# Moving two thirds of the mixers' early output product beside the second linear attention

## The chip, the cores and the metric

One core of one Trainium2 chip runs the whole program. The metric is device time in microseconds (us) of one execution; below is better. The engines in play are TensorE (PE, matmuls; PEld are its weight loads), VectorE (DVE), ScalarE (ACT), GpSimd (POOL) and SyncE (SP, which issues the weight loads from HBM).

## What is computed

A block of 512 tokens by 1024 features passes two attention and retention layers, a feed-forward, a layer of token mixers, a second feed-forward and a last norm. The change lies in the mixer layer only. Cut to what matters:

```
p_pool, p_hg, p_rw, p_gla = split(u @ w_in)
y_pool  = multiscale pooling(p_pool)            # 256 columns
y_hgrn  = chunked gated linear attention(p_hg)  # 256 columns, then norm and gate
y_rwkv  = rwkv7_scan(...)                       # 256 columns, then norm, bonus, gate
y_gla   = chunked gated linear attention(p_gla) # 256 columns, then norm and gate
x       = x + concat(y_pool, y_hgrn, y_rwkv, y_gla) @ w_out
```

The last line is a 512 x 1024 by 1024 x 1024 product. It splits over its contraction: each y contributes 256 of the 1024 rows of w_out, and the four contributions may be added to x at different times.

## The kernel before, in words

x is kept feature-major in eight tiles of 128 x 512. Every large product is done in three passes (`three_passes`, L447 to L450): operand and weight are each split in a rounded high part and a low rest, and high by high, low by high and high by low are summed in one PSUM bank of 128 x 512. Weights come in units of 128 x 1024 at most: SP loads one into a ring of four raw buffers, ACT writes its high part, DVE its low part, into rings of three. `use()` on ACT and DVE splits units up to two ahead of the one in use, and a unit's slot comes free when PE has signalled `weights used`.

The eight PSUM banks are handed out by turn in `take` (L417): a product takes the next bank in the turn, and PE waits there until the work named in `freed_by` has emptied it. So a slow reader of one bank stops PE eight takes later, whatever PE would do next.

Each engine has its own instruction stream, which runs in program order. The streams are written side by side with generators: a stage calls `fill(n)` at fixed points, and each engine advances the same generator there.

The mixer layer goes: projections for the pooling and the first attention (`hgrn`); `linear_attention("hgrn", fill_hgrn)`, with the second attention's (`gla`) projections as fillers; `linear_attention("gla", fill_gla)`; `inverse`; `recurrence`. A linear attention has nine levels (`ORDER` = 32, 16, 8, 4, 2, 1, 64, 128, 256). In each, DVE forms differences, ACT their exponentials, DVE the factors, PE the score products, and DVE (or ACT for 128 and 256) takes them from the banks. After the last level PE makes the values product ("mixed"). In `fill_gla` of before, n = 0 to 5 does the eight rwkv projections, n = 6 to 9 the steps of `operand_steps`: sigma and gate inputs and the key norm (n = 7), the token gate and the turned keys (n = 8), exponentials and operands after that. Its last DVE work is `rE`, for which PE's "bonus" product and all Gram products of `inverse` wait.

`inverse` builds a triangular inverse per head, bound by small matmuls. `recurrence` runs eight chunks: PE `carried` (4 matmuls) and the read of S, DVE `U`, PE `S step`, DVE `S`. In odd chunks PE also makes the output block ("M block") and DVE norms it (`finish_tile`). Between them stands a filler: eight output tiles f, each of 6 contraction tiles (pooling, hgrn, gla) by three passes, cut in two halves of nine passes; 13 halves are in the loop and three behind it. Their operands `y high` and `y low` are made at the start of `recurrence` from four PE transposes. After the loop the rwkv part follows ("mix last", 8 tiles of 6 passes), then `xg high`, `xg low` and the feed-forward.

Of the kernel before, what the change touches and what calls it, by code (L numbers as in the profile page):

```python
# [15 lines left out]
P = 128  # L16
# [33 lines left out]
ONE_PART = (2, 4, 6)  # L50
# [89 lines left out]
def unit_order(t):  # L140

    order = []
    for n in range(2):
        product = lambda g: [t["w_tok"][n, g, u] for u in range(4)]
        order += [t["w_rot"][n, f] for f in range(8)] + product(0) + product(1) + product(2)
        order += [t["w_qk"][n, f] for f in QK_ORDER] + [t["w_ag"][n, f] for f in range(4)]
        order += [t["w_out"][n, g, half, pair] for g, half, pair in OUT_STEPS]

    def feed_forward(which):
        units = [t["w_ffn_in"][which, f] for f in range(2 * FT)]  # L150
        return units + [t["w_ffn_out"][which, f][:, a:min(a + UNIT, D_FF)]
                        for f in range(KT) for a in range(0, D_FF, UNIT)]
# [12 lines left out]
    order += values[0:2] + projections[0:1]  # L165
    order += [values[2], projections[1], values[3]] + projections[2:]
    order += [t["w_mix_out"][f] for f in range(KT)] + [t["w_mix_out_rwkv"][u] for u in range(2)]
    return order + feed_forward(1)
# [17 lines left out]
class Memory:  # L186
# [71 lines left out]
    def mixers(self, region, rotary_at, xg_at, phase_at, end):  # L258
# [6 lines left out]
        m.pool_w = r.room("pool_w", 2, 64)  # L265
        m.y_pool = r.room("y_pool", 2, SEQ)
        m.ga = r.room("ga", SEQ)
        m.y_tok = {name: r.room(f"y_{name}", TT, G) for name in ("hgrn", "rwkv", "gla")}
        first_at = r.at
# [47 lines left out]
        m.y_high, m.y_low = (r.room(part, KT, SEQ, dt=F32R) for part in ("y_high", "y_low"))  # L317
# [91 lines left out]
def tensor_engine(e, s, mem, units):  # L409
# [315 lines left out]
    def mixers():  # L725
# [151 lines left out]
        projections, operand_prep = rwkv_steps(), operand_steps()  # L877

        def fill_gla(n):
            if n == 0:  # L880
                next(values_g)
                next(projections)
            elif n < 3:
                next(values_g)
                next(projections)
            elif n < 6:
                next(projections)
                if n > 3:
                    next(projections, None)
                if n == 5:  # L890
                    p.mark("xg read", MIX_NORM)
            else:
                next(operand_prep)

        linear_attention("gla", fill_gla)
        for _ in operand_prep:
            pass
# [91 lines left out]
    def recurrence(m):  # L989
        for name in ("hgrn", "gla"):  # L990
            for f in range(2):
                i = take(("turned y", name, f), ("y low", name, f))
                p.wait_ge(*of("y made", name))
                transposes(i, [m.y_tok[name][:, t, blk(f)] for t in range(TT)], "turned y", name, f)
        y_signal = [("y low", "pool", 0), ("y low", "pool", 1), ("y low", "hgrn", 0), ("y low", "hgrn", 1),
                    ("y low", "gla", 0), ("y low", "gla", 1)]

        def output_parts():
            for f in range(KT):
                i = take(("mix out", f), ("mix added", f))  # L1000
                held.add(i)
                n, high, low = next_unit()
                for k in range(6):
                    p.wait_ge(*of(*y_signal[k]))
                    last = three_passes(banks[i][:, :], (high[:, blk(k)], low[:, blk(k)]),
                                        (m.y_high[:, k, :], m.y_low[:, k, :]), k == 0, k == 5)
                    if k == 2:
                        yield
                last.then_inc(*p.up("weights used", n))
                p.mark("mix out", f)  # L1010
                held.discard(i)
                yield
# [3 lines left out]
        for c in range(n_chunks):  # L1016
# [14 lines left out]
            next(filler, None)  # L1031
# [20 lines left out]
            if c not in ONE_PART:  # L1052
                next(filler, None)
# [4 lines left out]
        for f in range(KT):  # L1058
            if f % 4 == 0:
                n, high, low = next_unit()  # L1060
            i = take(("mix last", f), ("out added", MIX_NORM, f))
            p.wait_ge(*of("y low", "rwkv", TT - 1))
            for k in range(2):
                c = blk(2 * (f % 4) + k)
                last = three_passes(banks[i][:, :], (high[:, c], low[:, c]),
                                    (m.y_high[:, 6 + k, :], m.y_low[:, 6 + k, :]), k == 0, k == 1)
            if f % 4 == 3:
                last.then_inc(*p.up("weights used", n))
                p.mark("mix last", f)
            else:  # L1070
                last.then_inc(*p.up("mix last", f))
# [15 lines left out]
def vector_engine(e, s, mem, units):  # L1087
# [117 lines left out]
    def rounded_low(low, value, high, *key):  # L1205
        v.wait_ge(*of("y high", *key))
        tt(low, value, high.bitcast(F32), ALU.subtract, "y low", *key)

# [214 lines left out]
    def mixers():  # L1423
# [202 lines left out]
        projections, operand_prep = rwkv_steps(), operand_steps()  # L1626

        def fill_gla(n):
            if n == 0:
                next(values_g)  # L1630
                finish_hgrn()
                next(projections)
            elif n < 3:
                next(values_g)
                next(projections)
            elif n < 6:
                next(projections)
                if n > 3:
                    next(projections, None)
            else:  # L1640
                next(operand_prep)

        finish_gla = linear_attention("gla", fill_gla)
        for _ in operand_prep:
            pass
# [57 lines left out]
    def recurrence(m):  # L1703
# [3 lines left out]
        for f in range(2):  # L1707
            rounded_low(m.y_low[:, f, :], m.y_pool[:, f, :], m.y_high[:, f, :], "pool", f)
        for k, (name, f) in enumerate((name, f) for name in ("hgrn", "gla") for f in range(2)):
            v.wait_ge(*of("y high", name, f))  # L1710
            stt(m.y_low[:, 2 + k, :], bank("turned y", name, f)[:, :], mem.col(name + "_norm", f), m.y_high[:, 2 + k, :],
                ALU.mult, ALU.subtract, "y low", name, f)

        def output_parts():
            for f in range(KT):
                use()
# [3 lines left out]
                yield  # L1720

        def finish_tile(t):
# [17 lines left out]
            part = (slice(None), slice(6, 8), blk(t))  # L1740
# [5 lines left out]
        for c in range(n_chunks):  # L1746
# [4 lines left out]
            next(filler, None)  # L1751
# [14 lines left out]
            if c not in ONE_PART:  # L1766
                next(filler, None)
# [29 lines left out]
def scalar_engine(e, s, mem, units, t):  # L1797
# [252 lines left out]
    def mixers():  # L2050
# [160 lines left out]
        projections, operand_prep = rwkv_steps(), operand_steps()  # L2211

        def fill_gla(n):
# [11 lines left out]
            else:  # L2225
                next(operand_prep)
                if n == 6:
                    bend_gate("gla")

# [6 lines left out]
        finish_gla = linear_attention("gla", fill_gla)  # L2236
        for _ in operand_prep:
# [44 lines left out]
    def recurrence(m):  # L2282
        fence("recurrence")
        small = mem.small
        for f in range(2):
            act(m.y_high[:, f, :], m.y_pool[:, f, :], "y high", "pool", f)
        for k, (name, f) in enumerate((name, f) for name in ("hgrn", "gla") for f in range(2)):
            a.wait_ge(*of("turned y", name, f))
            act(m.y_high[:, 2 + k, :], bank("turned y", name, f)[:, :], "y high", name, f,
                scale=mem.col(name + "_norm", f))  # L2290

        def output_parts():
            for f in range(KT):
                use()
                yield
                yield

        def finish_tile(i):
# [5 lines left out]
            part = (slice(None), slice(6, 8), blk(i))  # L2304
# [6 lines left out]
        for c in range(n_chunks):  # L2311
# [6 lines left out]
            next(filler, None)  # L2318
# [11 lines left out]
            if c not in ONE_PART:  # L2330
                next(filler, None)
# [28 lines left out]
def gpsimd_engine(e, s, mem, t):  # L2360
# [99 lines left out]

    def recurrence(m):
        fence("recurrence")
        bonus = mem.small[:, 112:128]
        for i in range(TT):
# [4 lines left out]
        tt(m.g_tok, m.g_tok, over_tiles(m.rows[:, 0, :]), ALU.mult, "gate ready")  # L2469
        pool_squares(NEXT_NORM[MIX_NORM])  # L2470
# [82 lines left out]
def layouts(inputs):  # L2553
# [7 lines left out]
    def groups(w):  # L2561
# [42 lines left out]
    out["w_mix_out"] = tiles(np.concatenate([w[0:512], w[768:1024]]))  # L2604
    out["w_mix_out_rwkv"] = tiles(w[512:768], 512).reshape(2, P, 2, 4, P).transpose(
        0, 1, 3, 2, 4).reshape(2, P, UNIT)
# [25 lines left out]
```

## Time and profile before

| | |
|---|---|
| median of 3 runs | 1811.35 us (1810.56 to 1811.60) |
| the profiled execution | 1811.65 us, of which the traced span is 1809.9 us |
| PE busy | 1728.1 us, 95% of the span |
| DVE busy | 873.9 us, 48% |
| ACT busy | 675.0 us, 37% |
| chain that ended last | PE 78%, DVE 14%, ACT 6%, issue 2% |

The page cuts the span in 40 slices of 45.2 us; a digit is a tenth. PEclk is the granted clock of TensorE, in tenths of 2.4 GHz. The stage that matters here is slices 26 to 31, from about 1140 to 1410 us. Matmuls overlap their records, so what counts for PE is the distance from start to start, not the duration of one record. An fp32 matmul shows as two records.

### The profile page before, as it was taken

What the parts mean: (1) busy time and instruction counts of PE and PEld (TensorE: products, weight loads), DVE (VectorE), ACT (ScalarE), POOL (GpSimd) and SP (SyncE); (2) the same over time, 40 slices, a digit from 0 to 9 for tenths busy, and PEclk for the clock granted to TensorE, in tenths of its full rate; (3) what the DMA queues carried; (4) which work ended last, traced back from release to release, by engine and by line L of the source; (5) the groups of instructions that cost most, each with busy time, mean ns of one, the idle gap of its engine ahead of it and who ended that gap; (6) DMA issues with size and microseconds to landing.
All of it is one profiled execution on the core that took longest, in us unless ns stands there. A gap on an engine that the chain in (4) does not pass through costs nothing.

```text
span 1809.9 us, 22171 instructions
## 1 busy us (share of the span) xinstructions
PE 1728.1 (95%) x8706; PEld 1406.9 (78%) x8706; DVE 873.9 (48%) x1171; ACT 675.0 (37%) x1016; POOL 130.9 (7%) x127
## 2 busy tenths in 40 slices
PE   7999999999999899999999989979998899999997
PEld 5777778778778688888887768869986678888885
DVE  5633444633445465444335765664345554444322
ACT  5145664225564333332223533363131433332221
POOL 0001001001001000000004000001320100000000
PEclk9999999999999999999999989966999899999998
DMA  5412213322212132223333211100001222223331
GB/s 180 132 68 71 82 59 104 118 81 80 80 52 82 58 117 93 93 97 93 96 99 128 80 50 55 60 9 1 1 18 47 81 82 96 102 97 96 96 96 47
DMA packets 41176, 143.91 MB, mean 80 GB/s; under 512 B 4864, under 2 KB 4880, under 8 KB 40816
## 3 DMA queue, kind: packets, MB, share of 16 engines
q1 hardware_dynamic: 37152, 130.61, 21.8%
q0 software_dynamic: 2192, 8.73, 1.5%
q10 hardware_dynamic: 1728, 3.15, 0.5%
q8 instruction: 69, 1.13, 0.3%
q14 instruction: 35, 0.29, 0.0%
HBM read 140.37 MB, written 2.10 MB: 79 GB/s over the span
## 4 chain that ended last, share of the span: by engine, by line
PE 78%; DVE 14%; ACT 6%; issue 2%; DMA 0%; POOL 0%; DVEq 0%; POOLq 0%; ACTq 0%; SPq 0%
PE bank L448 21%; PE bank L449 21%; PE bank L450 21%; PE bank L430 9%; DVE sb_w_low L1098 3%; DVE sb_E L1098 2%; PE bank L436 2%; ACT sb_E L1809 1%; DVE sb_near L1477 1%; PE bank L647 1%; PE bank L626 1%; PE bank L583 1%; ACT sb_w_high L1809 1%; ACT L1809 1%; DVE sb_rot L1098 1%
## 5 line engine op out<-in xcount | busy, mean ns | idle before, releaser
L448 PE MATMUL bank<-sb_xg_high,sb_w_high 128*128 128x512 f32 x1176 | 470.8, 400 | 29.3 <-DVE sb_xg_low L1106 18.2
L1098 DVE TENSOR_TENSOR sb_w_low<-sb_raw,sb_w_high 128x1024 fp32r<-128x1024 f32 (+1 forms) x253 | 311.5, 1231 | 382.9 <-ACT sb_w_high L1809 376.2
L450 PE MATMUL bank<-sb_xg_high,sb_w_low 128*128 128x512 f32 x1176 | 461.9, 393 | 0.0
L449 PE MATMUL bank<-sb_xg_low,sb_w_high 128*128 128x512 f32 x1176 | 461.8, 393 | 0.0
L1809 ACT ACTIVATE sb_w_high<-sb_raw 128x1024 fp32r<-128x1024 f32 (+1 forms) x253 | 263.2, 1040 | 355.7 <-PE bank L450 330.8
L448 PEld LDWEIGHTS bank<-sb_xg_high,sb_w_high 128*128 128x128 f32 x1176 | 223.1, 190 | 96.1 <-issue 35.6
L450 PEld LDWEIGHTS bank<-sb_xg_high,sb_w_low 128*128 128x128 f32 x1176 | 223.0, 190 | 47.9
L449 PEld LDWEIGHTS bank<-sb_xg_low,sb_w_high 128*128 128x128 f32 x1176 | 223.3, 190 | 45.7 <-issue 1.2
L448 PE MATMUL bank<-sb_h_high,sb_w_high 128*128 128x512 f32 x352 | 136.9, 389 | 0.0
L449 PE MATMUL bank<-sb_h_low,sb_w_high 128*128 128x512 f32 x352 | 136.9, 389 | 0.0
L450 PE MATMUL bank<-sb_h_high,sb_w_low 128*128 128x512 f32 x352 | 136.9, 389 | 0.0
L2369 POOL TENSOR_TENSOR sb_square_sum<-sb_square_sum,sb_square 128x512 f32<-128x512 f32 x35 | 45.0, 1286 | 969.0 <-ACT sb_square L1809 892.5
L448 PE MATMUL bank<-sb_w_high,sb_xg_high 128*128 128x512 f32 x256 | 103.1, 403 | 0.7 <-DVE sb_w_low L1098 0.7
L449 PE MATMUL bank<-sb_w_low,sb_xg_high 128*128 128x512 f32 x256 | 100.0, 390 | 0.0
L450 PE MATMUL bank<-sb_w_high,sb_xg_low 128*128 128x512 f32 x256 | 99.8, 390 | 0.0
L449 PEld LDWEIGHTS bank<-sb_h_low,sb_w_high 128*128 128x128 f32 x352 | 66.1, 188 | 13.8
L448 PEld LDWEIGHTS bank<-sb_h_high,sb_w_high 128*128 128x128 f32 x352 | 66.1, 188 | 13.7
L450 PEld LDWEIGHTS bank<-sb_h_high,sb_w_low 128*128 128x128 f32 x352 | 66.1, 188 | 13.6
L1809 ACT ACTIVATE sb_h_high<-sb_up 128x512 fp32r<-128x512 f32 x44 | 27.8, 632 | 117.8 <-DVE sb_up L1098 117.8
L1098 DVE TENSOR_TENSOR sb_up<-bank,sb_inv_rms 128x512 f32<-128x512 f32 x44 | 30.4, 692 | 80.2 <-PE bank L450 79.6
L1809 ACT ACTIVATE sb_gate<-sb_gate 128x512 f32<-128x512 f32 x44 | 27.8, 632 | 95.2 <-DVE sb_gate L1098 95.2
L448 PEld LDWEIGHTS bank<-sb_w_high,sb_xg_high 128*128 128x128 f32 x256 | 48.1, 188 | 19.5 <-issue 8.0
(332 smaller groups left out, 2129.9 us busy)
## 6 DMA issues: line engine op xcount, KB each, us to landing
sb_raw<-w_ffn_in SPq DMA_DIRECT2D x88, 512.0 KB, 3.2
sb_raw<-w_ffn_out SPq DMA_DIRECT2D x32, 512.0 KB, 3.5
sb_raw<-w_tok SPq DMA_DIRECT2D x24, 512.0 KB, 3.5
sb_raw<-w_mix_f SPq DMA_DIRECT2D x18, 512.0 KB, 3.2
sb_raw<-w_rot SPq DMA_DIRECT2D x16, 512.0 KB, 3.7
sb_raw<-w_qk SPq DMA_DIRECT2D x16, 512.0 KB, 3.2
sb_raw<-w_out SPq DMA_DIRECT2D x16, 512.0 KB, 3.2
sb_raw<-w_ffn_out SPq DMA_DIRECT2D x16, 384.0 KB, 3.1
```

What stands on the lines that cost most here:

```text
L430: made = e.matmul(out, lhsT, rhs, start=n == 0, stop=n == len(pairs) - 1)
L436: made = e.transpose(banks[i][:, blk(n)], in_, mem.ident)
L448: e.matmul(out, w[0], v[0], start=first, stop=False)
L449: e.matmul(out, w[0], v[1], start=False, stop=False)
L450: return e.matmul(out, w[1], v[0], start=False, stop=last)
L583: made = e.matmul(out[k], m.feat["rk"][r, f, blk(j)], m.feat["rq"][r, f, j * P:], start=part == 0, stop=part == 1)
L626: e.matmul(out[k], m.qT[r, j, blk(q)], m.kT[r, j, 0:keys], start=True, stop=True).then_inc(*p.up("scores", n, 2 * j + k, q))
L647: made = e.matmul(out[64 * k:64 * k + 64, blk(q)], m.tok["av"][:, key, h * ATT_DIM:(h + 1) * ATT_DIM], m.probT[:, 2 * (q % 2) + k, blk(key ...
L1098: e.tensor_tensor(out, a, b, op).then_inc(*v.up(*signal))
L1477: e.copy_predicated(near[:, :, :, size:], mem.pair_mask(size, 2 * TT).bitcast(I32), data).then_inc(*v.up("pairs taken", name, n, k))
L1809: e.activation(out, in_, func, bias=bias, scale=scale, accum_out=accum).then_inc(*a.up(*signal))
L2369: e.tensor_tensor(out, a, b, op).then_inc(*g.up(*signal))
```

## The change

The contribution of pooling and hgrn (4 contraction tiles) is taken out of the recurrence's filler and made during the last levels of the second attention. Its operands are rounded at the end of `fill_gla(4)`, hgrn's transposes with them. Eight "early out" tiles of 12 passes follow: two in fill 6, two in fill 7, two in fill 8, one in fill 9 and one behind the values product. DVE adds each to x one step later ("early added"). What is left in the recurrence is gla's contribution, 8 tiles of 6 passes: six in chunks 0 to 5, two behind the loop. The packing of the weights follows: 4 early units of 1024 columns, 2 for gla and 2 for rwkv, where before there were 8 of 768 and 2 of 1024. GpSimd's bonus, offset and gate operations move from the start of `recurrence` to the end of `inverse`.

```diff
-ONE_PART = (2, 4, 6)
+FILLED = 6
+EARLY = (("pool", 0), ("pool", 1), ("hgrn", 0), ("hgrn", 1))
+EARLY_STEPS = (2, 2, 2, 1)
```

The new filler on PE, and its place in `fill_gla` (n = 6 to 9) and behind the second attention, which is the same on PE, DVE and ACT:

```diff
+        def early_outputs():
+            for f in range(KT):
+                i = take(("early out", f), ("early added", f))
+                if f % 2 == 0:
+                    n, high, low = next_unit()
+                for k in range(4):
+                    p.wait_ge(*of("y low", *EARLY[k]))
+                    c = blk(4 * (f % 2) + k)
+                    last = three_passes(banks[i][:, :], (high[:, c], low[:, c]), m.early[k], k == 0, k == 3)
...
+                yield
...
             else:
+                for _ in range(EARLY_STEPS[n - 6]):
+                    next(early)
                 next(operand_prep)
...
         linear_attention("gla", fill_gla)
+        for _ in early:
+            pass
         for _ in operand_prep:
             pass
```

The same filler on DVE, and the roundings at the end of `fill_gla(4)` there (ACT makes the high parts, PE hgrn's transposes):

```diff
+        def early_outputs():
+            use()
+            yield
+            for f in range(KT):
+                v.wait_ge(*of("early out", f))
+                tt(x[:, f, :], x[:, f, :], bank("early out", f)[:, :], ALU.add, "early added", f)
+                if f % 2 and f < KT - 1:
+                    use()
+                yield
...
+            if n == 4:
+                for f in range(2):
+                    rounded_low(m.pool_low[:, f, :], m.y_pool[:, f, :], m.pool_high[:, f, :], "pool", f)
+                v.wait_ge(*of("turned y", "hgrn", 1))
+                for f in range(2):
+                    weighed_low(m.hgrn_low[:, f, :], m.hgrn_high[:, f, :], "hgrn", f)
```

PE's filler in the recurrence, and where its loop calls it:

```diff
         def output_parts():
             for f in range(KT):
...
+                late_product("mix out", f, ("mix added", f), [("y low", "gla", k) for k in range(2)], 0)
                 yield
...
-            next(filler, None)
+            if c < FILLED:
+                next(filler)
...
-            if c not in ONE_PART:
-                next(filler, None)
```

## Rows read from the trace of the kernel before

**Rows 1.** The page: granted clock of TensorE in 40 slices of 45.2 us.

```profile
PEclk9999999999999999999999989966999899999998
```

**Rows 2.** Busy windows: stretch, length, PE, PEld, DVE, ACT, POOL, clock, DMA, GB/s.

```profile
1150.00:1155.00 5.00, 5.00 (x23) 4.13 (x22) 3.86 (x6) 0.72 (x1) 0.00 (x0) 1.00 0.24 82
...
1184.29:1199.60 15.31, 15.31 (x69) 11.83 (x70) 8.62 (x11) 14.35 (x16) 2.93 (x1) 0.50 0.00 0
1210.60:1227.84 17.24, 17.09 (x81) 17.12 (x81) 9.98 (x11) 3.77 (x5) 0.00 (x0) 0.50 0.00 0
1227.84:1253.00 25.16, 25.16 (x111) 23.25 (x112) 8.86 (x13) 9.43 (x17) 2.55 (x2) 0.50 0.00 1
1256.00:1332.00 76.00, 75.25 (x625) 71.82 (x625) 29.11 (x54) 15.01 (x29) 22.80 (x18) 1.00 0.00 1
1333.90:1345.10 11.20, 9.15 (x35) 6.74 (x34) 9.80 (x10) 5.48 (x10) 10.10 (x6) 0.76 0.12 37
1345.10:1410.00 64.90, 56.92 (x304) 45.80 (x304) 35.75 (x74) 15.16 (x30) 0.00 (x0) 0.94 0.15 50
```

**Rows 3.** Timeline of PE: start, duration, line, operands; two passes after a gap.

```profile
1368.36 0.63 PE L450 MATMUL bank<-sb_y_high,sb_w_low 128*128 128x512 f32 x1
1368.78 0.63 PE L448 MATMUL bank<-sb_y_high,sb_w_high 128*128 128x512 f32 x1
```

**Rows 4.** Timeline of PE beside the last levels; brackets: idle before, and its releaser.

```profile
1184.29 3.78 PE L430 MATMUL bank<-sb_mixed,sb_lora 64*128 64x512 f32 x8 [7.36 <-ACT sb_mixed L1809]
1188.01 3.58 PE L430 MATMUL bank<-sb_mixer,sb_kI 128*128 128x2 f32 x16
1191.51 3.68 PE L762 MATMUL bank<-sb_E 64*128 64x64 f32 x32
...
1207.05 2.92 PE L430 MATMUL bank<-sb_E 64*128 64x256 f32 x8 [3.45 <-DVE sb_bI L1106]
...
1227.84 3.52 PE L430 MATMUL bank<-sb_mixer,sb_sigma 128*128 128x2 f32 x16
```

**Rows 5.** Timeline of DVE beside the second attention.

```profile
1158.41 1.23 DVE L1098 TENSOR_TENSOR sb_w_low<-sb_raw,sb_w_high 128x1024 fp32r<-128x1024 f32 x1
...
1202.40 2.49 DVE L1118 TENSOR_TENSOR_SCAN sb_cum<-sb_mixer,sb_sigma 128x512 f32<-128x512 f32 x2
...
1217.80 0.49 DVE L1102 TENSOR_SCALAR sb_tmp<-sb_a_gate,sb_cols 128x512 f32<-128x512 f32 x1
...
1223.12 1.22 DVE L1098 TENSOR_TENSOR sb_rE<-sb_mixed,sb_eB 128x1024 f32<-128x1024 f32 x1
```

**Rows 6.** Timeline of ACT: the high part of one unit.

```profile
1157.16 1.06 ACT L1809 ACTIVATE sb_w_high<-sb_raw 128x1024 fp32r<-128x1024 f32 x1
```

**Rows 7.** Timeline of PE in the recurrence and at mix last.

```profile
1339.31 0.50 PE L430 MATMUL bank<-sb_tokB,sb_tokA 64*128 64x128 f32 x2 [2.05 <-DVE sb_kkE L1098]
...
1354.19 0.65 PE L430 MATMUL bank<-sb_kI,sb_W2T 128*64 128x128 f32 x4
...
1359.71 0.65 PE L430 MATMUL bank<-sb_kI,sb_W2T 128*64 128x128 f32 x4 [1.08 <-DVE sb_kI L1098]
...
1367.05 0.66 PE L436 MATMUL bank<-sb_shared,sb_y_rwkv 128*128 128x128 f32 x2 [0.97 <-DVE sb_y_rwkv L1098]
...
1393.85 0.65 PE L430 MATMUL bank<-sb_kI,sb_W2T 128*64 128x128 f32 x4 [1.08 <-DVE sb_kI L1098]
...
1409.86 0.47 PE L448 MATMUL bank<-sb_y_high,sb_w_high 128*128 128x512 f32 x1 [1.31 <-DVE sb_y_low L1098]
```

**Rows 8.** Timeline of DVE in the recurrence's first two chunks and one later add.

```profile
1338.84 0.42 DVE L1098 TENSOR_TENSOR sb_kkE<-bank,sb_W 64x256 f32<-64x256 f32 x1
1339.36 2.80 DVE L1098 TENSOR_TENSOR sb_w_low<-sb_raw,sb_w_high 128x768 fp32r<-128x768 f32 x1
...
1346.84 0.96 DVE L1098 TENSOR_TENSOR sb_w_low<-sb_raw,sb_w_high 128x768 fp32r<-128x768 f32 x1
...
1354.30 0.69 DVE L1098 TENSOR_TENSOR sb_x<-sb_x,bank 128x512 f32<-128x512 f32 x1 [3.08 <-PE bank L450]
```

More of the change, by code:

```diff
@@ L875, in operand_steps @@
             yield
-        projections, operand_prep = rwkv_steps(), operand_steps()
+        def early_outputs():
[7 more added lines that the diff above has]
+                    last = three_passes(banks[i][:, :], (high[:, c], low[:, c]), m.early[k], k == 0, k == 3)
+                if f % 2:
+                    last.then_inc(*p.up("weights used", n))
+                    p.mark("early out", f)
+                else:
+                    last.then_inc(*p.up("early out", f))
+                yield
+        projections, operand_prep, early = rwkv_steps(), operand_steps(), early_outputs()
         def fill_gla(n):
@@ L892, in fill_gla @@
             else:
+                for _ in range(EARLY_STEPS[n - 6]):
+                    next(early)
                 next(operand_prep)
+            if n == 4:
+                for f in range(2):
+                    i = take(("turned y", "hgrn", f), ("y low", "hgrn", f))
+                    p.wait_ge(*of("y made", "hgrn"))
+                    transposes(i, [m.y_tok["hgrn"][:, t, blk(f)] for t in range(TT)], "turned y", "hgrn", f)
         linear_attention("gla", fill_gla)
+        for _ in early:
+            pass
         for _ in operand_prep:
@@ L989, in recurrence, with late_product @@
     def recurrence(m):
[L990 to L996, printed above, removed]
+        for f in range(2):
+            i = take(("turned y", "gla", f), ("y low", "gla", f))
+            p.wait_ge(*of("y made", "gla"))
+            transposes(i, [m.y_tok["gla"][:, t, blk(f)] for t in range(TT)], "turned y", "gla", f)
+        def late_product(key, f, freed_by, y_done, first_k):
+            if f % 4 == 0:
+                late[0] = next_unit()
+            n, high, low = late[0]
+            i = take((key, f), freed_by)
+            for k in range(2):
+                p.wait_ge(*of(*y_done[k]))
+                c = blk(2 * (f % 4) + k)
+                last = three_passes(banks[i][:, :], (high[:, c], low[:, c]),
+                                    (m.y_high[:, first_k + k, :], m.y_low[:, first_k + k, :]), k == 0, k == 1)
+            if f % 4 == 3:
+                last.then_inc(*p.up("weights used", n))
+                p.mark(key, f)
+            else:
+                last.then_inc(*p.up(key, f))
+        late = [None]
         def output_parts():
             for f in range(KT):
[L1000 to L1011, printed above, removed]
+                late_product("mix out", f, ("mix added", f), [("y low", "gla", k) for k in range(2)], 0)
                 yield
@@ L1058, in recurrence @@
         for f in range(KT):
[L1059 to L1071, printed above, removed]
+            late_product("mix last", f, ("out added", MIX_NORM, f), [("y low", "rwkv", TT - 1)] * 2, 2)
     def finish_tile(m, t):
@@ L1207, in rounded_low, with weighed_low @@
         tt(low, value, high.bitcast(F32), ALU.subtract, "y low", *key)
+    def weighed_low(low, high, name, f):
+        v.wait_ge(*of("y high", name, f))
+        stt(low, bank("turned y", name, f)[:, :], mem.col(name + "_norm", f), high.bitcast(F32), ALU.mult, ALU.subtract,
+            "y low", name, f)
     def added(n, f, factor):
@@ L1640, in fill_gla @@
             else:
+                for _ in range(EARLY_STEPS[n - 6]):
+                    next(early)
                 next(operand_prep)
+            if n == 4:
+                for f in range(2):
+                    rounded_low(m.pool_low[:, f, :], m.y_pool[:, f, :], m.pool_high[:, f, :], "pool", f)
+                v.wait_ge(*of("turned y", "hgrn", 1))
+                for f in range(2):
+                    weighed_low(m.hgrn_low[:, f, :], m.hgrn_high[:, f, :], "hgrn", f)
         finish_gla = linear_attention("gla", fill_gla)
+        for _ in early:
+            pass
         for _ in operand_prep:
@@ L1707, in recurrence @@
         for f in range(2):
[L1708 to L1712, printed above, removed]
+            weighed_low(m.y_low[:, f, :], m.y_high[:, f, :], "gla", f)
         def output_parts():
             for f in range(KT):
-                use()
+                if f % 4 == 0:
+                    use()
                 yield
@@ L2209, in operand_steps, with early_outputs @@
             yield
-        projections, operand_prep = rwkv_steps(), operand_steps()
+        def early_outputs():
+            use()
+            yield
+            for f in range(KT):
+                if f % 2 and f < KT - 1:
+                    use()
+                yield
+        projections, operand_prep, early = rwkv_steps(), operand_steps(), early_outputs()
         def fill_gla(n):
@@ L2225, in fill_gla @@
             else:
+                for _ in range(EARLY_STEPS[n - 6]):
+                    next(early)
                 next(operand_prep)
@@ L2228, in fill_gla @@
                     bend_gate("gla")
+            if n == 4:
+                for f in range(2):
+                    act(m.pool_high[:, f, :], m.y_pool[:, f, :], "y high", "pool", f)
+                for f in range(2):
+                    a.wait_ge(*of("turned y", "hgrn", f))
+                    act(m.hgrn_high[:, f, :], bank("turned y", "hgrn", f)[:, :], "y high", "hgrn", f,
+                        scale=mem.col("hgrn_norm", f))
         def preset(name, out, behind):
@@ L2236, in mixers @@
         finish_gla = linear_attention("gla", fill_gla)
+        for _ in early:
+            pass
         for _ in operand_prep:
@@ L2285, in recurrence @@
         for f in range(2):
[L2286 to L2290, printed above, removed]
+            a.wait_ge(*of("turned y", "gla", f))
+            act(m.y_high[:, f, :], bank("turned y", "gla", f)[:, :], "y high", "gla", f, scale=mem.col("gla_norm", f))
         def output_parts():
             for f in range(KT):
-                use()
-                yield
+                if f % 4 == 0:
+                    use()
                 yield
@@ L2459, in inverse @@
                     below(2 * size, h - 2)
-    def recurrence(m):
-        fence("recurrence")
         bonus = mem.small[:, 112:128]
+        g.wait_ge(*of("y made", "gla"))
+        g.wait_ge(*of("tokB", TT - 1))
         for i in range(TT):
```

41 lines of the change are left out of this document (25 added, 16 removed).

## The prediction

> **What bounds the kernel now.** I read the page first: PE is busy 95% of the span, yet in two slices its granted clock is 0.6 [rows 1]. Busy windows then show which work runs at 1.2 GHz: operand products and level 64 (1184 to 1200), the values product (1211 to 1228), and bonus and Gram products (1228 to 1253), all at 0.50 with PE nearly full [rows 2]. The PE timeline tells why: the clock is low after 7.36 us of idle waiting for ACT's tanh, and again from the 3.45 us before 1207.05 [rows 4]. So from 1166 to 1210 the path is not PE but the exchange of DVE and ACT over the levels, from 1210 to 1332 it is PE, and in the recurrence it is PE's filler (64.9 us, 56.9 busy) with DVE's `U` and `S` between [rows 2, 7].
>
> **Pass prices.** 22 passes start in 5.00 us: 0.227 us a pass at 2.4 GHz [rows 2]; 0.42 at 1.2 GHz [rows 3]. The product as a whole keeps its passes: 144 + 48 before, 96 + 48 + 48 after. 96 passes (21.8 us) leave the recurrence. If they fell wholly in idle PE time, that would be the gain. The question is what they hold up where they go.
>
> **Part 1, beside the last levels: +27 us.** The idle there (7.36 + 3.45 + about 1.7 in small gaps) is made by DVE and ACT, and the change puts work on exactly these two, in line:
> - Roundings in fill 4. ACT two of 0.65 and two of 0.69, DVE four of about 0.75, in front of DVE's take of level 4: DVE is busy back to back there, so +3.1. The same work leaves the recurrence (part 3).
> - Units of 1024 instead of 768 in fill 5, on ACT and DVE in turn: +0.75. The high part of one more unit (1.06 [rows 6]) stands before ACT's tanh, table loads and the exponentials of level 128: +1.1. The factors of level 128 are late by 5.0.
> - A bank. Counting the turns of `take` from the rwkv projections: early tiles 0 and 1 sit in the banks that the third and fourth of the sigma and gate inputs take, tile 2 in the second of level 64's, tile 3 in that of early tile 4, tiles 4 and 5 in the last two of level 128's. DVE adds a tile one step late, and tile 1 only after the factors of level 128, for which it waits for ACT. So PE finishes early tiles 0 to 3 by about 1189 at full clock, does three of the four inputs, and stands some 8.5 us until the add of tile 1 (1199.8). Then at half clock: last input 0.95, key norm 3.5, level 64 3.7 [rows 4]. Level 64's products end at about 1208 instead of 1195.2: +12.8.
> - The factors of the last level come 11.4 late (one ACT table load, 1.3, falls into the wait). Only then does DVE add tile 3, whose bank early tile 4 needs: 12 passes at half clock 5.1, and DVE waits for it before its scans. With two adds of 0.8 the scans, at 1202.40 before [rows 5], start +18.3. DVE's key scaling ends +19.6 with the wait for the turned keys.
> - The last head of level 128 waits for the add of tile 5, then the last level's products, ACT's copies and one more high part stand before ACT's rwkv exponentials: +22.5 for these.
> - PE goes on with early tile 6 (2.7), the values product, early tile 7 (2.7). Tile 4's dense passes should have brought the clock back, and the inverse shows such narrow matmuls holding it: 625 in 76.0 us, 0.122 each [rows 2]. So the values product takes 80 x 0.122 = 9.8 instead of 17.2. It is the one gain here.
> - **The cover that goes.** DVE's last operand steps (1217.80 to 1224.34, 6.5 us [rows 5]) were hidden under the values product. Now DVE's add of tile 7 stands before them, and PE makes tile 7 behind the values product. So PE idles add 0.8 + 6.5 before bonus. By this count bonus starts at 1253.7, not 1227.84 [rows 4]: +25.9. A gap of 1.7 before level 128's last head may lower the clock for a few us: +1. **Sum +27**, range 20 (waits kinder, all PE work at 2.4 GHz) to 36 (values product still at 1.2 GHz, +8).
>
> Bonus and Gram products follow an idle of 7 us as they do not now, but they already run at 0.50 for 25.16 us [rows 2]; I leave them unchanged.
>
> **Part 2, inverse: 0.** PE-bound (75.25 of 76.00 busy [rows 2]). GpSimd's 11 us now run at its end, where GpSimd is idle; nobody reads the gate before chunk 3. DVE's operations there read one operand from a bank. In the recurrence, a DVE split with two SBUF operands took 2.80 us while GpSimd ran and 0.96 later [rows 8], whereas `U`, with a bank operand, took 0.42 in the same stretch. From nothing to +1 for a slowed W2T.
>
> The Trainium skill (SBUF — State Buffer, Who interferes with whom) says a DVE instruction with two SBUF inputs contends with GpSimd's reads and one with at most one does not. By it the moved operations cost nothing in the inverse; the trace agrees so far.
>
> **Part 3, the recurrence: -14 us.** Count from the last W2T (1332.8) to mix last (1409.86 [rows 7]): 77.1 us before.
> - Start: `U` of chunk 0 stood behind six roundings, at 1338.84 [rows 8]; with two left it is at 1335.3. No GpSimd beside it, so the split of 2.80 and one `S` of 1.86 shrink to 1.2 and 0.4. Chunk 1 starts at 1338.7 instead of 1345.2.
> - Even chunks: 5.52 from 1354.19 to 1359.71 with a filler of nine [rows 7]. The path is carried, filler, S step, two DVE operations; six passes take 0.68 off: 4.84. Chunk 4 has a split too, 5.4.
> - Odd chunks: the second filler (2.3) goes too. Chunk 1 9.0 to 5.5; chunk 3 and 5 about 7.1 each (11.3 and 11.8 before), now set by the wait for DVE's norm of the tile.
> - Chunk 6 has no filler: 3.95. From chunk 7 to mix last 12.9 instead of 16.0 (1393.85 to 1409.86 [rows 7]): two tiles of six passes remain, and DVE's norm of the last tile and three adds of 0.69 [rows 8] are the path.
>
> That is 52.7 us, or -24.4, at 2.4 GHz throughout. But the clock: in this trace it was lowered after idles of 2.05 and 0.97 us [rows 3, 7], the stage had 0.94 on average with 88% busy [rows 2], and now PE is busy about 70% with the dense passes, which brought it back, cut to a third. With all of it at half clock the same path gives about 72 (-5). I take a bit under the middle of the gain, nearer to what happened beside narrow work: 63, -14. Range -24 to -5.
>
> **Part 4, after it: +1.** Mix last starts after waits of about 2.4 us twice, so probably at half clock; but its tiles are paced by DVE and ACT (eight tiles in 21 us), so only the first tile's passes (2.5 instead of 1.4) count. From 0 to +2.
>
> **Sum.** 1811.65 + 27 + 0 - 14 + 1 = 1825.65 for a profiled execution; the median stands 0.3 below it: **1825 us**, 0.8% slower.
>
> **Rivals.**
> 1. *The clock holds* (ends on the other side). The recurrence keeps 2.4 GHz (-24.4), and beside the levels the early passes keep the clock up, so that key norm, level 64 and early tile 4 take half of their 12 us: +20. With part 4 at 0 that is -4: 1807. If bonus and Gram products, too, ran at 2.4 GHz, 25.16 us would be halved: 1795. It decides for a gain once the waits of part 1 sum to less than 24 us. For it: dense passes did restore the clock each time. Against it: the 8.5 us wait for a bank and the 7.3 us before bonus are waits for DVE, whatever the clock.
> The Trainium skill (TensorE: Matmul & The Clock Gate, Why this matters for your kernels) warns only of the longer idle gaps between bursts of matmuls, so by it the recurrence's gaps of one to two us would leave the clock up, which is this rival's -24.4. The trace differs: the passes behind a gap of 0.97 us start 0.42 apart.
> 2. *Values product at half clock, recurrence mostly too*: +35 - 7 + 2 = +30, 1841. For it: the 0.50 of these stretches now. Against: early tile 6 is dense and stands directly before.
> 3. *The moved passes cost what they save* (the change does not do what it says): part 1 +20 to +22, part 3 about -20: within 0.2%, 1811.
>
> **How the numbers follow.** 0.2% (3.6 us) is about what a measurement of this kernel tells from no change. Forecast, 1816 to 1834: 0.55. Rival 2: 0.12. Rival 3: 0.10. Rival 1: 0.23. So faster 0.23, same 0.10, slower 0.67. The range leaves out the far half of rivals 1 and 2: 1803 to 1838.
>
> **What would show it.** In the profile of the changed kernel: an idle of PE of 7 to 9 us before the last gate input, ended by DVE's add on x; one of about 6 us before early tile 4, again by an add; one of about 7 us before bonus, ended by `rE`; values product at 0.11 to 0.12 us a matmul; bonus at 1248 to 1262. Between the last W2T and mix last 53 to 72 us, with a granted clock below 0.94. The prediction is wrong if ACT or DVE find slack for the early adds (then the shift before bonus is under 20 us), or if the recurrence holds clock 1.0.

## The result

| | before | changed |
|---|---|---|
| median | 1811.12 us (1810.56 to 1811.60) | 1821.41 us (1817.41 to 1822.28) |
| the profiled execution | 1811.65 us | 1822.04 us, span 1820.2 us |
| changed over before | | 1.0056, 95% interval 1.0045 to 1.0068 |

The change makes the kernel 10.3 us slower; 14 were forecast. The times of one kernel lie in groups: of 38 executions of the kernel before, taken beside the experiments, 11 are at 1807.8 to 1808.5 us with a mean granted clock of 0.967 or 0.968, the others at 1810.3 to 1812.4 with 0.963 to 0.965, and of the four of the changed kernel one (1817.41) has 0.967, the others 0.963.

The page of the changed kernel, busy time and granted clock:

```profile
PE 1723.4 (95%) x8706; PEld 1401.5 (77%) x8706; DVE 875.7 (48%) x1177; ACT 674.8 (37%) x1014; POOL 129.8 (7%) x127
...
PEclk9999999999999899999999989977998799999998
```

PE has less busy time than before (1723.4 us against 1728.1), and the span is 10.3 longer. So PE stands idle more. The two slices that had 0.6 [rows 1] now have 0.7. Slices 31 and 32, counted from one (1365 to 1456 us), at the recurrence and its end, had 0.9 and 0.8 and now have 0.8 and 0.7. Slice 14, which went from 0.9 to 0.8, lies some 500 us ahead of the change.

Timeline of PE in the changed kernel: every wait of over 0.9 us from the last gate input to bonus, and the values product (from 1234.58 to the first pass of early tile 7 at 1243.42):

```profile
1201.13 2.07 PE L444 MATMUL bank<-sb_mixed,sb_lora 64*128 64x512 f32 x2 [7.93 <-DVE sb_x L1130]
...
1216.78 0.80 PE L462 MATMUL bank<-sb_pool_high,sb_w_high 128*128 128x512 f32 x1 [6.47 <-DVE sb_x L1130]
...
1229.36 2.44 PE L444 MATMUL bank<-sb_E 64*128 64x128 f32 x20 [0.96 <-DVE sb_x L1130]
...
1234.58 1.22 PE L444 MATMUL bank<-sb_v_gla,sb_near 128*128 128x64 f32 x10
...
1243.42 0.48 PE L462 MATMUL bank<-sb_pool_high,sb_w_high 128*128 128x512 f32 x1
...
1253.81 3.58 PE L444 MATMUL bank<-sb_mixer,sb_sigma 128*128 128x2 f32 x16 [7.37 <-DVE sb_rE L1130]
```

Three waits end with DVE's add of an early tile to x, that is with a bank coming free. They take the place of the waits for ACT and for DVE's keys in [rows 4]. The fourth is for `rE`. Together they are 22.7 us.

Busy windows (stretch, length, PE, PEld, DVE, ACT, POOL, clock, DMA, GB/s) of the whole stage, from the first pass of the last two rwkv projections to bonus: the kernel before, then the changed one.

```profile
1162.03:1227.84 65.81, 53.29 (x299) 45.80 (x297) 40.91 (x45) 31.88 (x42) 2.93 (x1) 0.68 0.06 19
```

```profile
1164.01:1253.81 89.80, 66.48 (x395) 54.47 (x393) 54.21 (x61) 39.49 (x50) 2.93 (x1) 0.84 0.12 42
```

PE's idle time grows from 12.5 to 23.3 us, and its busy time by 13.2 us, less than the 21.8 us that 96 passes take, since the granted clock is higher (0.84 against 0.68).

Busy windows of the changed kernel: bonus to Gram's end; bonus to the last W2T (the end of DVE's last copy of the inverse's results out of its bank); last W2T to mix last; and of this, chunk 7 to mix last:

```profile
1253.81:1279.61 25.80, 25.80 (x113) 23.89 (x114) 9.45 (x13) 9.40 (x16) 2.55 (x2) 0.50 0.00 1
1253.81:1358.94 105.13, 105.13 (x759) 99.80 (x760) 41.26 (x69) 26.53 (x47) 35.60 (x27) 0.86 0.00 1
1358.94:1420.50 61.56, 47.12 (x243) 37.26 (x242) 34.00 (x76) 13.51 (x31) 0.00 (x0) 0.78 0.06 18
1401.13:1420.50 19.37, 11.98 (x40) 9.54 (x41) 9.96 (x24) 2.05 (x6) 0.00 (x0) 0.53 0.00 0
```

DVE's last W2T, before and changed:

```profile
1332.11 0.69 DVE L1102 TENSOR_SCALAR sb_W2T<-bank 64x512 f32<-64x512 f32 x1 [1.37 <-PE bank L430]
```

```profile
1358.25 0.69 DVE L1134 TENSOR_SCALAR sb_W2T<-bank 64x512 f32<-64x512 f32 x1 [1.37 <-PE bank L444]
```

The account, profiled execution against profiled execution: bonus starts 26.0 us later (1253.81 against 1227.84 [rows 4]; about 1 us of it is already there at 1165, ahead of the change). From bonus to the last W2T 105.1 us, against 105.0 before. From there to mix last 61.6 us instead of 77.1: -15.5. Behind mix last -0.2. Sum +10.4.

The last stretch, on PE and on DVE:

```profile
1401.13 1.12 PE L444 MATMUL bank<-sb_kI,sb_W2T 128*64 128x128 f32 x4 [1.07 <-DVE sb_kI L1130]
...
1413.56 0.79 PE L462 MATMUL bank<-sb_y_high,sb_w_high 128*128 128x512 f32 x1 [5.69 <-DVE sb_x L1130]
...
1420.50 0.47 PE L462 MATMUL bank<-sb_y_high,sb_w_high 128*128 128x512 f32 x1 [1.02 <-DVE sb_y_low L1130]
```

```profile
1412.29 0.42 DVE L1130 TENSOR_TENSOR sb_y_rwkv<-sb_y_rwkv,sb_offset 128x256 f32<-128x256 f32 x1
1412.82 0.69 DVE L1130 TENSOR_TENSOR sb_x<-sb_x,bank 128x512 f32<-128x512 f32 x1
1416.53 0.69 DVE L1130 TENSOR_TENSOR sb_x<-sb_x,bank 128x512 f32<-128x512 f32 x1 [3.02 <-PE bank L464]
1419.09 0.69 DVE L1130 TENSOR_TENSOR sb_x<-sb_x,bank 128x512 f32<-128x512 f32 x1 [1.87 <-PE bank L464]
1419.93 0.42 DVE L1130 TENSOR_TENSOR sb_y_low<-bank,sb_y_high 128x256 fp32r<-128x256 f32 x1 [0.16 <-ACT sb_y_high L1861]
```

DVE makes the add at 1412.82, that of output tile 5, only behind the whole norm of the last rwkv tile: tile 5 is made in chunk 5, its add is one filler step later, and chunks 6 and 7 have no filler. PE needs the bank that this add frees for tile 6 and stands 5.69 us; then the twelve passes of tiles 6 and 7 run at half clock, 5.3 us, before PE turns the last rwkv tile. The prediction had no such wait.

### The profile page after: what moved, and what is told of

It is laid out like the page before. It is cut to its first block, busy times and chain, and to the rows that moved or that the text cites. A ratio compares the mean times of both kernels' runs of the same rounds, so it can differ in the third digit from the quotient of the medians.

```text
span 1820.2 us, 22177 instructions
## 1 busy us (share of the span) xinstructions
PE 1723.4 (95%) x8706; PEld 1401.5 (77%) x8706; DVE 875.7 (48%) x1177; ACT 674.8 (37%) x1014; POOL 129.8 (7%) x127
## 4 chain that ended last, share of the span: by engine, by line
PE 78%; DVE 13%; ACT 5%; issue 2%; DMA 0%; DVEq 0%; POOLq 0%; POOL 0%; ACTq 0%; SPq 0%
PE bank L462 21%; PE bank L463 21%; PE bank L464 21%; PE bank L444 9%; DVE sb_w_low L1130 2%; DVE sb_E L1130 2%; PE bank L450 2%; ACT sb_E L1861 1%; DVE sb_near L1514 1%; PE bank L661 1%; PE bank L640 1%; PE bank L597 1%; ACT sb_w_high L1861 1%; DVE sb_rot L1130 1%; DVE sb_x L1138 1%
## 5 line engine op out<-in xcount | busy, mean ns | idle before, releaser
L463 PEld LDWEIGHTS bank<-sb_h_low,sb_w_high 128*128 128x128 f32 x352 | 66.1, 188 | 13.6
```

Source lines behind the costliest of these rows:

```text
L463: e.matmul(out, w[0], v[1], start=False, stop=False)
```

## The experiments

Theory: the loss is waits, not passes. They are bank waits behind adds that DVE makes one step late, and the wait for `rE`, whose operand steps stand behind DVE's add of tile 7. Rival: the passes themselves, or the clock, set the time. "After" in the expectations is the changed kernel. Those of x5 to x8 were written with the results of x1 to x4 at hand. The kernel before stood at 1811.32 us beside x1 to x4 and at 1810.84 beside x5 to x8; differences to the changed kernel are of medians, and by the ratios they come out within 2.3 us of that. The 95% intervals of x5, x6 and x4 overlap that of the changed kernel; for these three the traces carry the argument.

### Adds one step earlier (x2_adds_on_time)

On DVE and ACT, not on PE:

```diff
+ADD_STEPS = (3, 2, 2, 1)
...
-                for _ in range(EARLY_STEPS[n - 6]):
+                for _ in range(ADD_STEPS[n - 6]):
```

> The changed kernel, with VectorE's adds of the early tiles (and the weight splits between them, on ScalarE too) one step earlier: three steps in fill 6 instead of two. Theory (PE waits for banks that VectorE empties one step late): the 7.9 us wait before the last gate input and the 6.5 us wait before early tile 4 go or shrink to what the second bank of level 64 still waits (tile 2's add), scans start 8 to 9 us earlier, bonus 10 to 12 us earlier: about 1810. Rival (VectorE and ScalarE have no slack, the chain of levels itself is what is late): the waits change places, no more than 3 us is won, 1818 to 1821.

Measured: 1813.71 us (1810.87 to 1815.19), 1.0018 (1.0008 to 1.0027). Timeline of PE:

```profile
1202.28 3.68 PE L777 MATMUL bank<-sb_E 64*128 64x64 f32 x32 [4.86 <-DVE sb_x L1131]
...
1221.21 2.92 PE L445 MATMUL bank<-sb_E 64*128 64x256 f32 x8 [2.50 <-DVE sb_bI L1139]
...
1248.03 3.58 PE L445 MATMUL bank<-sb_mixer,sb_sigma 128*128 128x2 f32 x16 [7.37 <-DVE sb_rE L1131]
```

Instead of 7.93 and 6.47 us PE waits 4.86 us for an add, and early tile 4 doesn't wait. Waits of 0.97, 1.60 and 2.50 us appear in other places, so bonus starts 5.8 us earlier (1248.03), not the 10 to 12 that were expected. The kernel gains some 7 us against the changed one (7.7 by the medians, 6.9 by the ratios): adds one step earlier win back most of the net loss of 10.3. The wait for `rE` is 7.37 to the hundredth, as it was: DVE's last steps start when PE is done with tile 7, wherever that lies.

### Operand steps ahead of the last adds (x1_dve_last, x3_both)

DVE alone, x1_dve_last; x3_both is the same with ADD_STEPS:

```diff
         finish_gla = linear_attention("gla", fill_gla)
-        for _ in early:
-            pass
+        next(early)
         for _ in operand_prep:
             pass
+        for _ in early:
+            pass
         inverse(m, finish_gla)
```

> The changed kernel, with VectorE's last operand steps put ahead of its add of early tile 7 (the add of tile 6 stays where it is). Theory (the cover is gone): the operand steps run beside the values product again, rE ends at about 1249 instead of 1253.8, PE waits about 2 to 3 us for it instead of 7.4, and the time falls by 5 to 6 us, to about 1816; if the shorter wait leaves the clock at 2.4 GHz, bonus and Gram products (26.2 us at half clock) give another 10 to 13 us, 1804. Rival (the wait before bonus is only the visible end of a chain of bank waits): nothing or 1 us, 1820 to 1821.

Measured: 1817.09 us (1809.90 to 1819.13), 1.0030 (1.0017 to 1.0042). Bonus waits 2.57 us for `rE` instead of 7.37:

```profile
1248.01 3.57 PE L444 MATMUL bank<-sb_mixer,sb_sigma 128*128 128x2 f32 x16 [2.57 <-DVE sb_rE L1130]
```

That is the cover that the prediction saw go. Bonus starts 5.8 us earlier, but 1.0 of this is there at the last gate input already (1200.15 against 1201.13), ahead of the edit: putting the cover back gives 4.8 us there, 4.3 in the medians and 4.7 by the ratios.

```profile
1251.60:1275.00 23.40, 23.40 (x102) 21.51 (x103) 10.61 (x14) 10.29 (x18) 2.55 (x2) 0.50 0.00 1
```

This window of it, behind bonus, is still at 0.50: the wait of 2.57 us did not leave the clock up either, so the part of the expectation that hung on it did not come.

> Both edits of x1 and x2 together. Theory: rE is ready as early tile 7 ends, PE does not stop before bonus, bonus starts some 18 us earlier than in the changed kernel and runs with the Gram products at 2.4 GHz (another 10 to 13 us): about 1791, range 1788 to 1800. Rival (the clock of the Gram stage has nothing to do with the wait before it): -18 alone, 1803.

Measured: 1813.48 us (1810.97 to 1815.27), 1.0016 (1.0006 to 1.0025): nothing beyond x2_adds_on_time. The edit was at fault, not the theory. With one add more in the fillers, the one step let ahead of the operand steps is tile 7's add itself, so DVE still waited for PE, and bonus still shows 7.37 us for `rE`:

```profile
1247.23 3.57 PE L445 MATMUL bank<-sb_mixer,sb_sigma 128*128 128x2 f32 x16 [7.37 <-DVE sb_rE L1131]
```

### Both, with all operand steps first (x7_both_mended)

As x3_both, without the `next(early)`.

> x2's early adds, and VectorE's operand steps ahead of the add of early tile 7. (In x3 the order was as in x2: with the adds moved up, the one step that x3 let go ahead of the operand steps was the add of tile 7 itself.) In x2's trace kkE and the two products after it end at 1233.6 and tile 7 at 1240.6, so the remaining 6.5 us of operand steps end at 1240.1: PE no longer waits before bonus, which starts at about 1240.8 instead of x2's 1248.0. Theory: -7 against x2 at the least, 1806.5; if the clock holds into the Gram products up to 12 more, 1795. Rival (another wait takes its place, as for a bank that the add of tile 7 empties): 1811 to 1813.

Measured: 1800.15 us (1798.90 to 1801.74), 0.9945 (0.9929 to 0.9962): faster than before. Timeline of PE (level 64; early tile 7; bonus; the third head's Gram products; the second product of the inverse), then of ACT:

```profile
1202.38 3.68 PE L777 MATMUL bank<-sb_E 64*128 64x64 f32 x32 [4.85 <-DVE sb_x L1131]
...
1237.78 0.47 PE L463 MATMUL bank<-sb_pool_high,sb_w_high 128*128 128x512 f32 x1
...
1240.63 1.84 PE L445 MATMUL bank<-sb_mixer,sb_sigma 128*128 128x2 f32 x16
...
1249.59 1.16 PE L445 MATMUL bank<-sb_kkE,sb_bI 64*128 64x128 f32 x8 [1.12 <-DVE sb_XT L1717]
...
1261.23 1.10 PE L445 MATMUL bank<-sb_Pm,sb_XT 128*128 128x64 f32 x8 [3.78 <-ACT sb_Pm L1862]
```

```profile
1260.28 0.21 ACT L1862 ACTIVATE sb_small<-sb_small 128x16 f32<-128x16 f32 x1 [2.37 <-DVE sb_small L1147]
1260.58 1.28 ACT L1862 ACTIVATE sb_Pm<-bank 128x512 f32<-128x512 f32 x2
```

Windows: the stage up to bonus; bonus and Gram; bonus to the last W2T; and a part of the inverse's first products:

```profile
1164.05:1240.63 76.58, 66.19 (x395) 54.93 (x394) 53.49 (x60) 39.49 (x50) 2.93 (x1) 0.87 0.14 49
1240.63:1255.50 14.87, 13.75 (x114) 12.68 (x112) 7.39 (x11) 9.05 (x16) 2.55 (x2) 1.00 0.00 1
1240.63:1338.91 98.28, 93.38 (x760) 88.69 (x759) 40.77 (x70) 26.51 (x47) 35.64 (x27) 0.98 0.00 1
1262.18:1265.46 3.28, 3.28 (x18) 3.28 (x18) 2.03 (x3) 0.00 (x0) 0.00 (x0) 0.54 0.00 0
```

Bonus now follows the last pass of tile 7 without a wait, 7.4 us earlier than in x2_adds_on_time. And bonus and Gram products run at 1.00, in 14.9 us instead of 25.8. Of these 10.9 us 4.1 are given back at once. PE comes to the inverse's second product before ACT has copied `Pm`, since a small operation ahead of it on ACT waits 2.37 us for DVE's norm of the attention. PE idles 3.78 us; the first product, now at full clock, is 1.4 us shorter, which leaves 2.4. Behind the wait the clock is at half for some 3 us (0.54), which costs another 1.7. So 98.3 us from bonus to the last W2T instead of 105.1. The 7.4 us up to bonus and the 6.7 from there to the last W2T (105.0 in x2_adds_on_time), less 0.9 us that the recurrence takes more, make 13.2 of the 13.6 us between the medians of x7_both_mended and x2_adds_on_time.

### The clock alone (x5_clock_held)

The changed kernel with 30 dense passes more, into bonus's bank ahead of its wait; bonus overwrites them, so nothing else is computed.

```diff
             i = take(("bonus",), ("bonus",))
+            for _ in range(30):
+                e.matmul(banks[i][:, :], m.hgrn_high[:, 0, blk(0)], m.hgrn_high[:, 1, :], start=True, stop=True)
             p.wait_ge(*of("rE"))
```

> The changed kernel, with 30 dense passes of 128x512 on PE (6.8 us at 2.4 GHz) into the bonus product's own bank ahead of the wait for rE; bonus overwrites them, nothing reads them. They fill the 7.4 us in which PE stood. Theory A (the wait before bonus lowers the clock for the whole of bonus and Gram products): these run at 2.4 GHz, about 13 instead of 26 us, time 1808 to 1810. Theory B (bonus, two columns wide, and the Gram products, 64 rows high, don't hold the clock by themselves): the clock falls inside them, 2 to 8 us won, 1813 to 1819. Theory C (the clock there is set by the kind of products, whatever came before): 1821.

Measured: 1815.91 us (1812.48 to 1823.48), 1.0038 (1.0022 to 1.0054). The ten times fall in two groups, five from 1812.5 to 1813.0 and five from 1818.8 to 1823.5; the profiled one (1812.74) is of the first. Its PE timeline and windows:

```profile
1244.48 6.96 PE L884 MATMUL bank<-sb_hgrn_high 128*128 128x512 f32 x30
1252.01 1.95 PE L444 MATMUL bank<-sb_mixer,sb_sigma 128*128 128x2 f32 x16 [0.57 <-DVE sb_rE L1132]
...
1261.08 1.16 PE L444 MATMUL bank<-sb_kkE,sb_bI 64*128 64x128 f32 x8 [1.12 <-DVE sb_XT L1718]
...
1264.58 2.08 PE L444 MATMUL bank<-sb_kkE,sb_bI 64*128 64x128 f32 x8
```

```profile
1252.01:1263.30 11.29, 10.17 (x82) 9.39 (x83) 3.46 (x5) 7.62 (x13) 1.83 (x2) 1.00 0.01 1
1263.30:1270.06 6.76, 6.76 (x33) 6.21 (x32) 6.00 (x9) 1.79 (x3) 0.72 (x1) 0.51 0.00 0
1252.01:1349.55 97.54, 96.42 (x759) 91.66 (x760) 41.28 (x69) 26.53 (x47) 35.44 (x27) 0.95 0.00 1
```

Bonus lies within 0.5 us of where it lay (this run is 1.3 us ahead from the last gate input on), and 7.6 us are gained from bonus to the last W2T, by the clock: the same bonus product takes 1.95 us instead of 3.58. Some 2 us behind the 1.12 us wait for `XT` the clock falls, and the rest of the Gram products run at 0.51. This is the expectation's theory B, with theory A right up to that wait. The upper group of times is some 6 to 11 us longer, with a mean granted clock of 0.963 to 0.967 against 0.969. That is about what the clock gives here; where it fell in those executions was not traced.

### Tiles in chunks 6 and 7 too (x6_filled8, x8_all)

```diff
-FILLED = 6
+FILLED = 8
```

> The changed kernel with FILLED = 8: the last two of gla's output tiles run in chunks 6 and 7 instead of behind the loop. In the changed kernel's trace tile 6 waited 5.7 us for a bank that VectorE empties only after the norm of the last rwkv tile, and both tiles then ran at half clock, with VectorE's last rounding behind their adds. Theory: that stretch, 19.4 us from chunk 7 to mix last, goes to about 14, chunk 6 gets up to 1 us longer: 1816 to 1818. Rival (the norm of the last tile is the path whatever the tiles do): 1820 to 1822.

Measured: 1816.50 us (1816.11 to 1817.64), 1.0039 (1.0024 to 1.0054). Windows: last W2T to mix last; chunk 7 to mix last; then PE's timeline, the turn of the last rwkv tile and mix last:

```profile
1357.76:1413.19 55.43, 41.95 (x243) 32.59 (x242) 34.01 (x75) 13.50 (x31) 0.00 (x0) 0.89 0.06 20
1401.04:1413.19 12.15, 5.73 (x34) 4.27 (x35) 9.28 (x23) 2.05 (x6) 0.00 (x0) 0.79 0.00 1
```

```profile
1411.51 0.66 PE L450 MATMUL bank<-sb_shared,sb_y_rwkv 128*128 128x128 f32 x2 [4.95 <-DVE sb_y_rwkv L1130]
1413.19 0.76 PE L462 MATMUL bank<-sb_y_high,sb_w_high 128*128 128x512 f32 x1 [1.02 <-DVE sb_y_low L1130]
```

The last stretch takes 12.15 us instead of 19.37, at 0.79 instead of 0.53. PE still waits 4.95 us for the norm, but no passes stand behind it any more. Chunks 0 to 6 take 1.1 us more, with a tile in chunk 6 too. Behind mix last 1.6 us are given back (401.3 us to the end instead of 399.7): the first passes there now run at half clock (0.76 us, against 0.47 in the changed kernel). Net -4.5 from the last W2T to the end in the profiled executions, -4.9 in the medians.

> x7 and x6 together. Theory: the two lie in different stretches and add up: x7's time less 4 to 5 us, about 1802 (1790 with the clock held), below both kernels. Rival (the recurrence's clock falls more often with fillers spread over all chunks): no better than x7.

All three edits: 1796.79 us (1794.21 to 1798.41), 0.9928 (0.9913 to 0.9943). It beats before by 14 us and the changed kernel by 24.6, and x7_both_mended by 3.4, where 4 to 5 were expected. Window of bonus and Gram, and last W2T to mix last:

```profile
1239.62:1257.59 17.97, 16.86 (x113) 15.51 (x112) 10.14 (x14) 9.41 (x16) 2.55 (x2) 0.82 0.00 1
...
1337.05:1392.60 55.55, 42.02 (x244) 32.63 (x242) 34.01 (x75) 13.50 (x31) 0.00 (x0) 0.89 0.06 20
```

Here the clock falls 2 us behind the wait for `XT`, and yet bonus to W2T is 97.4 us, not longer than in x7_both_mended. The second product of the inverse has no wait for `Pm` here: the slower Gram products fill it.

```profile
1261.01 1.10 PE L445 MATMUL bank<-sb_Pm,sb_XT 128*128 128x64 f32 x8
```

### GpSimd's work put back (x4_pool_back)

Bonus, offset and gate operations on GpSimd again at the start of `recurrence`; all else as in the changed kernel.

> The changed kernel, with GpSimd's offset and gate operations back at the start of the recurrence. Theory: VectorE's split and one S update with two SBUF operands are slowed as before (2.8 and 1.9 us instead of 1.2 and 0.4 at most), so chunk 1 starts 2 to 3 us later: 1823 to 1824. Rival: they meet no such operation at the new places, or chunk 1 has slack: no difference, 1821.

Measured: 1824.67 us (1823.06 to 1825.87), 1.0078 (1.0063 to 1.0093). Timeline of DVE in chunk 0, x4_pool_back first, then the changed kernel:

```profile
1362.10 2.89 DVE L1130 TENSOR_TENSOR sb_w_low<-sb_raw,sb_w_high 128x1024 fp32r<-128x1024 f32 x1 [0.69 <-ACT sb_w_high L1861]
...
1365.65 1.82 DVE L1130 TENSOR_TENSOR sb_kI<-sb_kI 128x256 f32<-128x256 f32 x1
```

```profile
1362.57 1.23 DVE L1130 TENSOR_TENSOR sb_w_low<-sb_raw,sb_w_high 128x1024 fp32r<-128x1024 f32 x1 [0.70 <-ACT sb_w_high L1861]
...
1364.46 0.43 DVE L1130 TENSOR_TENSOR sb_kI<-sb_kI 128x256 f32<-128x256 f32 x1
```

GpSimd works from 1358.79 to 1369.67 there. The split loses 1.66 us and `S` 1.39: 3.05, and 3.3 in the medians. So this part of the change is a gain of about 3 us by itself. In the inverse GpSimd's operations cost nothing that is seen (bonus to the last W2T 105.1 us with them there and 105.1 in x4_pool_back without).

The Trainium skill (SBUF — State Buffer, Who interferes with whom) says that a DVE instruction with two SBUF inputs contends with a GpSimd instruction that reads SBUF. The trace agrees: 2.89 and 1.82 us beside GpSimd, 1.23 and 0.43 without. The times read like a wait for the operation under way: the split, begun at 1362.10, ended 1.09 us behind the GpSimd operation of 1361.55 to 1363.90, and the next GpSimd operation took 3.20 us, against 2.35 in the changed kernel. Between the two, `S`'s first add, with a bank operand, took 0.42.

## Why the prediction was right, and where it was not

**Part 1, +27 forecast, +26 measured** (some 25 without the offset at the start). Its steps held, most of them within 1 us. The wait before the last gate input, 8.5, was 7.93, and ended with the add of tile 1 at 1200.38 (1199.8). The wait before early tile 4, about 6, was 6.47. The scans began at 1222.81, +20.4 instead of +18.3: 1.0 is the offset at the start, and the last gate input took 2.0 us at half clock instead of 0.95 (0.95 was its share of four in a row). The values product took 8.8 us instead of 9.8: the one gain, right in kind. The gap before bonus, 7.3, was 7.37. Bonus at 1253.81, forecast 1253.7; that the two agree to 0.1 us is luck, since misses of 1 to 2 us both ways cancel. x2_adds_on_time (5.8 us) and x1_dve_last (4.8 us) show the two kinds of wait to be causes, not company. Without most of both, in x7_both_mended, bonus is at 1240.63: 13.2 us earlier. What then remains, 12.8 us over before, is less than the 21.8 us of passes, but little of that is idle time filled: PE's idle time in the stage is 10.4 us there against 12.5 before. The rest is the clock (0.87 against 0.68), 8.2 us in the values product alone.

**Bonus and Gram, 0 forecast.** Right for this kernel, since they ran at 0.50 before and after. But I left them out of the sum as unchanged, and in x7_both_mended they are worth 7 us: the wait for `rE` cost its own length, and the clock was low behind it.

**Part 2, 0 forecast.** Right, 105.13 us against 105.0. Taking GpSimd out of the recurrence's start had its share in part 3: the 3 us of x4_pool_back.

**Part 3, -14 forecast, -15.5 measured: the sum near, a term of it wrong.** The start held: `U` of chunk 0 stands 2.5 us behind the last W2T, and chunk 1 starts 6.1 behind it (5.9). I had 52.7 us at 2.4 GHz and took 63, the 10 us between for the clock. Chunks 0 to 6 took 42.2 us, only 2.4 over their full-clock sum of 39.8; chunk 1 took 7.1 instead of 5.5 and chunk 6 5.0 instead of 3.95, each with half clock behind a wait. The step that failed is "from chunk 7 to mix last 12.9": it took 19.4. I counted the norm and the adds, but not that tile 6, the first of the two behind the loop, takes a bank which DVE frees behind that norm: 5.69 us of waiting, and then twelve passes at half clock on the path. x6_filled8, where tiles 6 and 7 are made in chunks 6 and 7, takes 12.15 there and 55.4 in all, 2.7 over the full-clock sum. So of the 10 us that I gave to the clock, some 6 were this wait with what follows from it, and that 63 came near 61.6 is luck: the allowance for the clock paid for a wait that I had not seen. The method that found the banks in part 1, counting turns of `take`, wasn't used for part 3.

**Part 4, +1 forecast, -0.2 measured.** Small, but not for the reason given. I had mix last start at half clock, and it started at full clock (0.47 us at 1420.50). In x6_filled8 it does start at half clock, and the part is 1.6 us longer than in the changed kernel.

**The rivals.** Rival 1 took its point from the sum of the waits, under 24 us. They came to 22.7 in this kernel, and it is slower, so the mark was wrong: it set the waits of part 1 against all 24.4 us of part 3 at full clock, and part 3 gave 15.5, while the shift of part 1 was 26, more than its waits. Its second mark, bonus and Gram at 2.4 GHz, was right as a mechanism: in x7_both_mended it comes about. Of the 12.6 us that halving would give, the stage shows 10.9 and the end 6.8. Rival 2 fell with the values product at 8.8 us, rival 3 with part 1 at +26.

## What to carry to other kernels

When work is moved into another stage of a kernel whose buffers go round by turn, count the turns for each new tenant: who frees it, and behind what that engine has queued. A reader one step late cost some 7 us here, and one behind a norm 5. Put the work that the next stage waits for ahead of adds that nobody waits for. Look at PE's clock behind each wait: taking away a wait of 7 us gave nearly 7 more in narrow matmuls behind it. And look for who is late next; ACT's late copy of `Pm`, with the clock behind it, took back 4.1 of 10.9.

## What the runs showed of the hardware

The bonus and Gram products (128x2, and 64 rows by 128 columns) did not raise the clock. In the changed kernel bonus and Gram products began at 0.50 behind 7.37 us of idle, and were still at 0.50 after 25.8 us with PE busy all the time. In x7_both_mended the same 113 or so matmuls ran at 1.00 throughout, behind dense passes without a gap. Not every narrow product is like this: the inverse's first, 128 rows by 128 columns, still ran at half in the changed kernel (3.4 us from 1279.61), and the one behind it was at full clock.

A wait of 1.12 us inside them had no fixed result. In x7_both_mended the clock stayed at 1.00 behind it; in x5_clock_held and x8_all it was halved about 2 us later. What decides isn't settled by these runs, and x5_clock_held's two groups of times may be the same matter. The longer waits, 2.57 us before bonus in x1_dve_last, 3.78 in x7_both_mended and 7.37 in the changed kernel, were each followed by half clock. Of idle gaps, the Trainium skill (TensorE: Matmul & The Clock Gate, Why this matters for your kernels) warns of the longer ones between bursts only. The trace agrees for the 7.37 us and differs for the 1.12 us in two of three kernels.
